# A decoder step with 32 experts: samples gathered in bf16 parts, the last four experts out of the loop, single transfers at both ends of the weight ring

## What is computed

```python
def moe(xf, w_router, b_router, w1, b1, w2, b2):
    logits = xf.astype(F32) @ w_router.astype(F32) + b_router.astype(F32)
    top_v, top_e = lax.top_k(logits, TOP_K)          # 4 of 32
    gates = jax.nn.softmax(top_v, axis=-1)
    ...
    def run_block(args):
        e, toks, g = args
        xb = xf[toks]
        h = xb @ w1[e] + b1[e]                       # 1024 x 2048
        glu = jnp.minimum(h[:, ::2], SWIGLU_LIMIT)
        lin = jnp.clip(h[:, 1::2], -SWIGLU_LIMIT, SWIGLU_LIMIT)
        a = glu * jax.nn.sigmoid(SWIGLU_ALPHA * glu) * (lin + 1)
        out = a @ w2[e] + b2[e]                      # 1024 x 1024
        return out * g[:, None].astype(out.dtype)
    ...
x1 = layer_norm(DN_ALPHA * x + mix, ln1_g, ln1_b)
ff = moe(x1.reshape(B * T, D), ...).reshape(B, T, D)
x2 = layer_norm(DN_ALPHA * x1 + ff, ln2_g, ln2_b)
y = x2 + jax.nn.sigmoid(x2 @ w_ple_gate) * (p.astype(x2.dtype) @ w_ple)
```

## Time and profile before

| | us |
|---|---|
| three runs, median (lowest, highest) | 1114.68 (1113.35, 1115.1) |
| the profiled execution | 1113.78 |
| its span | 1112.0 |
| TensorE busy | 1096.1 |
| VectorE busy | 409.0 |
| ScalarE busy | 165.3 |
| GpSimd busy | 78.7 |
| DMA over the span, mean | 396 GB/s |

### The profile page before, as it was taken

One profiled execution on the slowest core, in us unless ns is written; L12 is line 12 of the kernel. 1 busy time (PEld: TensorE's weight loads), 2 busy tenths in 40 slices (PEclk: granted clock), 3 DMA queues, 4 the chain that ended last, 5 costly groups with the idle time before them and its releaser, 6 DMA issues.

```text
span 1112.0 us, 14748 instructions
## 1 busy us (share of the span) xinstructions
PE 1096.1 (99%) x5674; PEld 423.5 (38%) x5674; DVE 409.0 (37%) x881; ACT 165.3 (15%) x310; POOL 78.7 (7%) x103
## 2 busy tenths in 40 slices
PE   8999999999999999999999999999999999999998
PEld 6886433333333333333333333333333333332344
DVE  1737763333333333333333333333333333323255
ACT  1622330001000100010001000100001000100043
POOL 0847410000000000000000000000000000000000
PEclk9999999999999999999999999999999999999999
DMA  9988889999999999999999999999999999999971
GB/s 315 266 314 336 255 336 421 426 427 427 430 427 430 427 430 427 428 429 427 429 429 428 429 428 428 427 431 427 428 429 428 429 428 428 427 430 428 428 282 39
DMA packets 48723, 440.43 MB, mean 396 GB/s; under 512 B 10513, under 2 KB 13837, under 8 KB 23766
## 3 DMA queue, kind: packets, MB, share of 16 engines
q1 hardware_dynamic: 47657, 437.43, 94.9%
q0 software_dynamic: 896, 2.66, 0.7%
q10 hardware_dynamic: 148, 0.07, 0.0%
HBM read 436.61 MB, written 3.77 MB: 396 GB/s over the span
## 4 chain that ended last, share of the span: by engine, by line
PE 81%; DMA 11%; SPq 5%; DVE 2%; POOL 1%; issue 0%; ACT 0%; DVEq 0%; POOLq 0%
PE bank L904 36%; PE bank L946 18%; DMA ring<-in_w_mlp 9%; PE bank L843 7%; PE bank L865 5%; PE bank L1022 3%; PE bank L708 2%; PE bank L878 2%; PE bank L928 2%; SPq L356 1%; PE bank L891 1%; POOL ring L1912 1%; PE bank L935 1%; PE bank L871 1%; PE bank L538 1%; DMA q_row<-srow 1%
## 5 line engine op out<-in xcount | busy, mean ns | idle before, releaser
L904 PE MATMUL bank<-ring,proj 128*64 128x512 f32 x2048 | 466.0, 597 | 4.5 <-DMA ring<-in_w_mlp 4.5
L1429 DVE SCALAR_TENSOR_TENSOR xT<-bank,proj,xT 128x512 f32<-128x512 f32 x128 | 90.2, 747 | 440.9 <-PE bank L865 439.6
L904 PEld LDWEIGHTS bank<-ring,proj 128*64 128x64 f32 x2048 | 135.5, 136 | 288.2 <-issue 247.4
L946 PE MATMUL bank<-ring,wpool 128*64 128x512 f32 x1024 | 225.1, 592 | 0.0
L946 PEld LDWEIGHTS bank<-ring,wpool 128*64 128x64 f32 x1024 | 71.2, 137 | 129.9 <-issue 129.0
L1777 ACT ACTIVATE proj<-proj 128x256 f32<-128x256 f32 x64 | 26.7, 416 | 546.5 <-DVE proj L1458 546.5
L843 PE MATMUL bank<-xreg,proj 128*64 128x512 f32 (+1 forms) x396 | 95.4, 599 | 0.1
L538 PE MATMUL bank<-xT,ring 128*128 128x264 f32 x320 | 73.9, 388 | 1.7 <-DMA ring<-in_w_in 1.7
L865 PE MATMUL bank<-mixT 64*128 64x512 f32 x264 | 74.5, 641 | 0.5 <-ACT mixT L1785 0.5
L538 PEld LDWEIGHTS bank<-xT,ring 128*128 128x128 f32 x320 | 60.0, 190 | 13.4 <-issue 3.4
L1785 ACT COPY mixT<-bank 128x512 f32<-128x512 f32 x32 | 18.7, 585 | 232.3 <-PE bank L946 232.3
(11 more groups left out here) (334 smaller groups left out, 624.7 us busy)
## 6 DMA issues: line engine op xcount, KB each, us to landing
ring<-in_w_mlp SPq DMA_DIRECT2D x192, 2048.0 KB, 23.5
ring<-in_w_in SPq DMA_DIRECT2D x10, 1024.0 KB, 13.6
ring<-in_w_out SPq DMA_DIRECT2D x4, 1024.0 KB, 8.3
ring<-in_w_ple_gate SPq DMA_DIRECT2D x4, 1024.0 KB, 28.0
xreg<-in_x_prompt SPq DMA_DIRECT2D x4, 512.0 KB, 4.3
ring<-q_row SPq DMA_DIRECT2D x1, 2048.0 KB, 6.9
ring<-k_row SPq DMA_DIRECT2D x1, 2048.0 KB, 6.7
out<-ring POOLq DMA_DIRECT2D x1, 2048.0 KB, 17.6
```

Of the source, the lines that this page charges most:

```text
L904: last = pe.matmul(bank[q][BLOCK * t:BLOCK * (t + 1), :], xgT[:, k % 4, k // 4, :], ring[:, s, col:col + 512], start=False, stop=(k == KD ...
L946: last = pe.matmul(bank[4][BLOCK * h:BLOCK * (h + 1), :], aT[:, m, BLOCK * t:BLOCK * (t + 1)], w[:, k % 2, 512 * h:512 * h + 512], start=F ...
L1429: ins = STT(total[:, c, s], ins_bank[h][:, :], gate_table[:, c, bass.ds(n, 1)], total[:, c, s], ALU.mult, ALU.add)
```

## The change

**The samples' part of the gather.** The 8 sample rows of x1 are written once, ahead of the loop, as three bf16 parts whose sum is the f32 row: in rows 0 to 7, 32 to 39 and 64 to 71 of a bf16 view of `xtok[:, 2]`, whose first 512 columns VectorE clears early by a memset. ScalarE casts, GpSimd subtracts, in a chain. The one-hot of this chunk is a bf16 matrix of 96x64, made by one more instruction per expert on VectorE. The gather of the samples is then two bf16 matmuls over 96 rows in place of two f32 ones over 8. The very first gather stays as it was. TensorE waits for the parts (`sample_moved` 11) ahead of the gather in the first expert of each body, ScalarE ahead of its loop.

**The loop.** It runs over 28 experts on each engine; the last four are written out behind it. The last one has no gather, no spread, no turning of gathered rows, no one-hot and no copy of gathered rows.

**The transfers.** Pair 16 is loaded as two transfers of 1 MB, the first when one unit is used, the second when two are. In the last expert the pairs of units 6, 7 and 10, 11 are two transfers of 1 MB each, with the waits of a pair, and TensorE waits for each unit.

Some semaphores are merged (`ident_in` into `x_in0`, `sn_ready` into `srow_ready`), `num_ps` is gone.

```diff
+        sample_parts = xtok[0:3 * 32, 2, :].bitcast(BF16)[:, 0:D]
+        part_high = sig.rearrange("p q f -> p (q f)")[0:SAMPLES, :].bitcast(BF16)
+        part_mid = act_out[0:SAMPLES, :].bitcast(BF16)
...
             for n in range(SLOTS, UNITS * STEP, 2):
-                sp.wait_ge(sem("units_used"), n - SLOTS + 2)
-                load_next(n)
+                if n == SLOTS:
+                    for a in range(2):
+                        e, u = divmod(n + a, UNITS)
+                        s = slot_of(n + a)
+                        sp.wait_ge(sem("units_used"), a + 1)
+                        sp.dma_start(ring[:, s, :], unit_weights(e, u)).then_inc(sem(f"slot{s}"), 16)
+                else:
+                    sp.wait_ge(sem("units_used"), n - SLOTS + 2)
+                    load_next(n)
+            def load_body(e, done, closing=False):
...
+                    single = closing and j == STEP - 1 and u in SINGLES
                     sp.wait_ge(sem("units_used"), done + (n - SLOTS + 2))
+                    if single:
+                        for a in range(2):
+                            s = slot_of(n + a)
+                            sp.dma_start(ring[:, s, :], unit_weights(e + j, u + a)).then_inc(sem(f"slot{s}"), 16)
+                    else:
+                        load_pair(e + j, j, u)
...
+                        if c < 2 or n is None:
+                            where, rows_ = onehot[0:m, c, 0:BLOCK], xtok[0:m, c, 512 * h:512 * h + 512]
+                        else:
+                            where, rows_ = onehot16, sample_parts[:, 512 * h:512 * h + 512]
+                        last = pe.matmul(bank[2][BLOCK * h:BLOCK * (h + 1), :], where, rows_, start=(c == 0), stop=(c == 2))
...
-                pe.wait_ge(sem("onehot_ready"), n * 2 + 4)
-                gather(n + 1)
-                pe.wait_ge(sem("hotT_done"), n + 1)
-                spread_places((j + 1) % 2)
+                if not final_one:
+                    if j == 0:
+                        pe.wait_ge(sem("sample_moved"), 11)
+                    pe.wait_ge(sem("onehot_ready"), n * 3 + 5)
+                    gather(n + 1)
+                    pe.wait_ge(sem("hotT_done"), n + 1)
+                    spread_places((j + 1) % 2)
...
-            with pe.Fori(0, npass * EXPERTS, STEP) as n:
+            with pe.Fori(0, npass * EXPERTS - STEP, STEP) as n:
                 for j in range(STEP):
                     expert(n + j, j)
+            for j in range(STEP):
+                expert(npass * EXPERTS - STEP + j, j, True)
...
             dve.wait_ge(sem("mem_ps"), 2)
+            dve.memset(xtok[:, 2, 0:D // 2], 0.0).then_inc(sem("rest_cleared"), 1)
...
+                if chunks == 2:
+                    TT(onehot16, cst[0:3 * 32, C_SLOT:C_SLOT + BLOCK],
+                       pos_table[0:3 * 32, 2, bass.ds(n, 1)].to_broadcast([3 * 32, BLOCK]), ALU.is_equal)\
+                      .then_inc(sem("onehot_ready"), 1)
...
+            act.wait_ge(sem("ple_ps"), 3)
+            act.copy(part_high, xtok[0:SAMPLES, 2, :]).then_inc(sem("part_cast"), 1)
+            for q in range(1, 3):
+                act.copy(pos_table[32 * q:32 * q + SAMPLES, 2, :], pos_table[0:SAMPLES, 2, :])\
+                   .then_inc(sem("sample_moved"), 1)
+            act.wait_ge(sem("part_rest"), 1)
+            act.copy(part_mid, xtok[0:SAMPLES, 2, :]).then_inc(sem("part_cast"), 1)
+            act.wait_ge(sem("part_cast"), 2)
+            act.copy(sample_parts[32:32 + SAMPLES, :], part_mid).then_inc(sem("sample_moved"), 1)
+            act.wait_ge(sem("part_rest"), 2)
+            act.copy(sample_parts[0:SAMPLES, :], part_high).then_inc(sem("sample_moved"), 1)
+            act.wait_ge(sem("sample_moved"), 11)
             act.wait_ge(sem("passes_ready"), 1)
             npass = act.value_load(extra[0:1, 0:1], min_val=0, max_val=PASSES - 1) + 1
...
+            rows_ = xtok[0:SAMPLES, 2, :]
+            pool.wait_ge(sem("sample_begun"), 1)
+            pool.wait_ge(sem("gathered"), 1)
+            pool.wait_ge(sem("part_cast"), 1)
+            pool.tensor_tensor(rows_, rows_, part_high, ALU.subtract).then_inc(sem("part_rest"), 1)
+            pool.wait_ge(sem("part_cast"), 2)
+            pool.tensor_tensor(sample_parts[64:64 + SAMPLES, :], rows_, part_mid, ALU.subtract).then_inc(sem("part_rest"), 1)
             pool.wait_ge(sem("total_ready"), 2)
```

More of the change, by code:

```diff
@@ L471, in _ @@
             used = npass * (EXPERTS * UNITS)
+            load_body(last, used - STEP * UNITS, True)
             def wait_slot(s):
@@ L879, in turn_gathered, with landed, expert @@
                 last.then_inc(sem("xgT_ps"), 1)
-            def expert(n, j):
+            def landed(u, i4, closing):
+                s = slot_of(u)
+                if closing and u // UNITS == STEP - 1 and (u % UNITS) // 2 * 2 in SINGLES:
+                    seen = landings(u) if u % 2 == 0 else 1
+                    pe.wait_ge(sem(f"slot{s}"), i4 * 12 + 16 * (before[s] + seen) if u % 2 == 0 else 16 * (before[s] + 1))
+                elif u == SLOTS + 1:
+                    pe.wait_ge(sem(f"slot{s}"), 16 * (before[s] + 1))
+                elif u % 2 == 0:
+                    pe.wait_ge(sem(f"slot{s}"), i4 * 12 + 16 * (before[s] + landings(u)))
+            def expert(n, j, closing=False):
                 i4 = n - j
+                final_one = closing and j == STEP - 1
                 pe.wait_ge(sem("xgT_done"), n + 1)
@@ L895, in expert @@
                     s = slot_of(u)
-                    if k % 2 == 0:
-                        pe.wait_ge(sem(f"slot{s}"), i4 * 12 + 16 * (before[s] + landings(u)))
+                    landed(u, i4, closing)
                     if k == 5:
@@ L940, in expert @@
                     s = slot_of(u)
-                    if k % 4 == 0:
-                        pe.wait_ge(sem(f"slot{s}"), i4 * 12 + 16 * (before[s] + landings(u)))
+                    if k % 2 == 0:
+                        landed(u, i4, closing)
                     w = ring[:, s, :].rearrange("p (a f) -> p a f", a=2)
@@ L1511, in _ @@
             dve.wait_ge(sem("gates_table"), 1)
-            with dve.Fori(0, npass * EXPERTS, STEP) as n:
+            with dve.Fori(0, npass * EXPERTS - STEP, STEP) as n:
                 for j in range(STEP):
                     expert(n + j, j)
+            for j in range(STEP):
+                expert(npass * EXPERTS - STEP + j, j, j == STEP - 1)
             done = npass * (3 * EXPERTS)
```

83 lines of the change are left out of this document (49 added, 34 removed).

## The result

| | median us (lowest, highest), runs | profiled execution | its span | mean granted clock |
|---|---|---|---|---|
| before | 1114.86 (1113.35, 1116.54), 18 | 1113.78 | 1112.0 | 0.999 |
| after | 1116.64 (1114.93, 1118.53), 18 | 1116.81 | 1115.0 | 0.997 |

The ratio is 1.0016, 95% interval 1.001 to 1.0023: 1.8 us more, within 0.2%. Edit 1, edit 2 and edit 3 are the prediction's: pair 16 as two single transfers; the samples' gather in bf16 and its preparation; the last four experts outside the loop, with single transfers ("singles") at units 6 and 10 of the last one.

The account below looks back on a forecast made before the run. The prediction took the full DMA queue from pair 24 on as the bound. Preparation with pair 16's singles +1.2, last expert -0.84 and -0.12, sum +0.2 us: 1114.9 against the median 1114.68, range 1112.4 to 1117.0.

Parts of the forecast that it names:

- the sigmoid: Sign in expert 0: ScalarE's first sigmoid would come near 170 us and not 167.9.
- pair 24's landing: Sign at the head: the 2 MB weight pair from which the queue stays full lands near 186, not 184.8.
- What bounds the kernel: From pair 24 on the DMA queue never rests; its fill time, 179 intervals and TensorE's work after the last landings set the end.
- Rival (c): In the loop: TensorE is the bound, 0.72 us saved counts in 31 experts: -22, 1092 us; chance 0.02.
- Edit 1, -0.4: At the head: pair 16 as singles starts 1.8 us earlier, but pair 24's landing comes forward by only 0.4 us.
- Edit 2's preparation, +1.6: Ahead of the loop: ScalarE casts and GpSimd subtractions make VectorE's first product 1.6 us later; +1.2 with the singles included.
- rival (b): In the preparation: GpSimd's subtractions, possibly held up by VectorE, take 3.2 us each: +1.5, 1116.2 us; chance 0.2.
- Gather, memset, VectorE's one-hot, small moves, 0: Loop gather's saved 0.72 us becomes waiting; the memset and extra compare are covered by VectorE's idle time: 0 at the end.
- Edit 3, -0.96: In the last expert: singles remove a 0.84 us wait, and L878's absence gives 0.12.
- Fetched code, 0: Code outside the loop must be fetched; forecast without a gap, 0, a stall mostly covered by TensorE's 0.9 us reserve per expert.
- Landings, 179 intervals of 4.90: From pair 24 to the last pair, weight pairs land 4.90 us apart, with that period unchanged.

Follow-up runs that it names:

- before and after again: The unchanged kernel and the kernel with all three edits, each run once more without alteration: 1114.77 (ratio 1.0) and 1116.87 us (1.0023).
- the three casts: Three more ScalarE casts of 8x1024 ahead of the first one, against all three edits plus unread matmuls in the last expert's gather place: 1119.76 us, ratio 1.0039.
- experiment 5: Kernel before with only pair 16 as two singles: 1115.41 us, ratio 1.0008; with only the bf16 gather and its preparation: 1116.81 us, ratio 1.0014.
- edit 2 alone: Kernel before with only the samples' bf16 gather, its preparation and the memset added: 1116.81 us, ratio 1.0014.
- no edit 2, filler: Changed kernel with the samples' gather back in f32, no preparation, and unread matmuls in the last expert's gather place: 1114.55 us, ratio 0.9996.
- the early load: All three edits, unread matmuls in the last expert's gather place, ScalarE's pass-count load moved ahead of its casts: 1114.71 us (0.9997), again 1114.84 (1.0001).
- no edit 2: Changed kernel with the samples' gather in f32 as before, no bf16 parts and no memset: 1116.95 us, ratio 1.0019.
- filler: Changed kernel plus six f32 matmuls of 512 columns, output unread, where the last expert's gather stood: 1116.28 us, ratio 1.0009.

## Why the prediction was right, and where it was off

The forecast was +0.2 us, within 0.2%, in 1112.4 to 1117.0; it is +1.8, within 0.2%, at 1116.64. The two traces without a slow front, before and after again, give the exact sum: +0.02 in the copies, +0.74 to pair 24's issue, +0.73 to the last landing, -1.09 for the tail with its clock kept (49.45 against 50.54), +1.56 for the slow clock (51.01 against 49.45). Together +1.96: 1113.95 - 1111.99.

That the time lies in the range is in part luck. Four terms were off: edit 1 (0 for -0.4), the preparation (+0.74 for +1.6), the landings (+0.73 for 0) and the clock of the tail (+1.56 for 0). Three made the kernel slower than forecast, the preparation quicker; with the preparation at its 1.6 the same median would have been 1117.5, outside the range. Two of the signs came out by luck too: in the first trace the sigmoid at 170.12 (forecast near 170) and pair 24's landing at 185.9 (near 186) hold 1.07 us of the slow stretch at 9.6; in the second, which has none in the front, they are 169.2 and 185.3.

- **What bounds the kernel** held. Delays of pair 24 came out at the end, the three casts above all; 0.72 us less matmul per expert came out nowhere. Rival (c) is refuted by the measured time itself, by the 0.72 us of waiting in a middle expert, and by the kernels with the f32 gather, which aren't slower.
- **Edit 1, -0.4:** wrong; no gain shows, and the single runs hint at a cost (experiment 5). The step failed where it took the quicker of two lone transfers (8.2 us) as what an early start buys. A landing is the last of 16 parts. The trace has the times at which the 16 parts are added to the pair's semaphore. In thirteen of the fourteen traces the ninth of the sixteen is there 7.2 to 7.4 us after pair 24's issue, and the last 7.8 to 9.8 (in the one with edit 2 alone 8.2 and 10.6). The landing of a lone pair is scattered by its slowest part, and 8.2 and 9.1 look like two draws from that, not a price of singles: pair 24 took 7.76 to 9.77, mean 8.5, in the ten traces with edit 1, and 8.55 to 8.72 in three of the four without it. (The Trainium skill, "DMA: Bandwidth & Descriptors", Why a DMA increments its semaphore by 16 and not by 1, says that a transfer runs on up to 16 engines that finish independently, each adding 1; by that the trace agrees, though it doesn't name the engines.) The prediction's estimate of 6.8 us for a pair was by the same page of the Trainium skill, whose section "Anatomy of one DMA" is about transfers issued by GpSimd, and these are SyncE's; none of the fourteen landings of pair 24 took less than 7.76.
- **Edit 2's preparation, +1.6:** right in mechanism and sign, twice too large. Measured +0.74 to pair 24's issue. The term that was off is the subtraction: 2.12 us against 2.55, twice, 0.86. The bare register load was 0.96 and 1.11 against 0.8. That GpSimd is held up by VectorE, rival (b), didn't show: the two subtractions took 2.12 and 2.13. But it was hardly put to the test, since VectorE's one-hots met only the last 0.2 us of the first subtraction. Where they met it fully, with three more casts, it was VectorE that was held (last section).
- **Gather, memset, VectorE's one-hot, small moves, 0:** right.
- **Edit 3, -0.96:** the singles gave 1.04 for 0.84, L878's absence nothing for 0.12. What failed is the sentence that behind L928 "only what is behind it counts". That TensorE idles there was read off correctly, and idling was taken as free. It cost 1.56 to 1.67 us in the granted clock of the matmuls after it, more than the singles gained. No term of the prediction, no rival and no bound of the range had it. This is the largest miss.
- **Fetched code, 0:** 0 in the changed kernel's own two traces, whose landings step only before the unrolled part. It was 1.5 in one trace of the same tail (no edit 2, filler), 0.3 in two more (at 924.7 and 931.5), and 0.4 and 0.6 just ahead of the last landings in the two with the early load. So not always 0.
- **Landings, 179 intervals of 4.90:** off by 0.73 in this pair. Steps of 0.2 to 1.2 us stand in every trace but that of edit 2 alone, mostly one or two between 195 and 270. Each of these follows one of the four 16 KB code fetches between 189 and 270 by 2 to 5 us; not every such fetch is followed by a step. That the fetch makes the step is the likely reading, and no run tested it. The kernel before has them too (0.37 in one trace, 0.28 and 0.78 in the other). The step of the changed kernel at 196.4 follows this one (DMA view, 191 to 193):

```profile
q8 instruction: 1, 0.02, 3.1%
```

**What stays open:** whether the change itself makes the landings later, by the unrolled code or by edit 1. Without unrolled code the stretch from issue to last landing is 885.2 to 886.7 (five traces, mean 885.8), with it 885.6 to 887.6 (nine, mean 886.3); these overlap. A kernel with the code laid out so that no fetch falls into the full queue wasn't tried. Nor was a filler in the front.

**No version beats both.** All three edits, the filler and the early register load are 2.0 us quicker than the changed kernel and even with the one before (0.9997 and 1.0001). The account gives it 1.2 us less than the one before (0.08 at the head, 1.09 at the tail). From the copies to the end its two traces have 954.08 and 954.26, those of the kernel before 954.61 and 955.14, so 0.4 to 1.1 us are there, and later landings take the rest; the medians don't show them.

## What to carry to other kernels

Where work is taken off TensorE ahead of a wait, ask what the granted clock does afterwards: 2.5 to 2.9 us of idling cost the matmuls behind it another 1.6 us, at two places in this case (the last expert, and expert 0 with three more casts). Work that nobody reads is worth leaving in, if it ends before the wait does. When a kernel is bound by a full transfer queue, as here, look first at what moves the pair from which it is full and at what follows the last landings. Where two kernels differ by less than such slow stretches cost, compare runs with the same mean clock. Move also the small register loads that engines do between stages: one that had been hidden behind copies stood bare and cost 0.7.

## What the runs showed of the hardware

- **The clock** of the identical kernel falls or stays by run. Before again fell to 0.50 at 41.1 us, the first trace of before didn't, though the work there is the same. Ahead of the tail's projections it fell in the three traces with 2.84 to 2.88 us of idling, and stayed in those with the filler, with 0.28 to 0.33. In expert 0 it fell after 2.52 and stayed after 1.41 to 1.55. It fell only 1.1 to 1.9 us after TensorE had begun to work again, so the price is paid by what comes behind the wait.
- **The 16 parts of a pair drift apart and stay so.** Their increments for one pair keep the same distances over hundreds of us: in the changed kernel the ninth is 1.83 us ahead of the last at 276 and 1.87 at 902, the fifteenth 0.15 and 0.23. The steps of the landings stay to the end; a small delay of the last part, 0.12 at 917, was gone at 927. Of the fetches of the unrolled code between 916 and 1048, none moved the landings of the changed kernel for good, though the distances of the others changed (the ninth 1.87 ahead at 902, 1.73 at 981). In the kernel without edit 2 and with the filler fourteen of the fifteen are suddenly 1.1 us further ahead at 1002, and the fifteenth 0.66. That fits a fetch that met the engine which was already the last; the trace doesn't name the engine.
- **GpSimd's subtraction** of 8x1024 took 2.12 us with f32 as well as with bf16 output, and VectorE's work beside it made no difference; for 128x512 it took 1.26, so twice the columns cost 0.86 more.
- **Which of the two is held.** In the kernel with three more casts VectorE's compare of two SBUF operands began 0.8 us after GpSimd's subtraction. It took 1.50 us where it takes 0.36 in the changed kernel, and ended 0.16 after the subtraction, which took its 2.12; a product beside the second subtraction took 0.97 for 0.43. In the earlier trace rows VectorE had begun first, and GpSimd's copy was the long one. In these three meetings the one that began first went on. GpSimd, then VectorE, in the timeline of that kernel:

```profile
164.70 2.12 POOL L2045 TENSOR_TENSOR xreg<-xreg,proj 8x1024 f32<-8x1024 f32 x1 [7.32 <-ACT proj L1871]
165.48 1.50 DVE L1456 TENSOR_TENSOR proj<-cst,proj 128x128 f32<-128x128 f32 x1 [2.00 <-ACT proj L1873]
```
